# Bias rows of a two-block model, written in 24 pieces during the first layer's feed-forward

## The reference

```
s = einsum(q, k) * Dh**-0.5 + bias[rel_pos];  masked;  softmax
```

## Time and profile before

| | |
|---|---|
| median of 3 runs | 1955.09 us |
| lowest, highest | 1953.01, 1956.92 us |
| profiled execution | 1958.29 us |
| its span | 1955.80 us |
| TensorE busy | 1879.0 us (96%) |
| VectorE busy | 1169.9 us (60%) |
| ScalarE busy | 884.6 us (45%) |
| GpSimd busy | 90.3 us (5%) |
| mean granted TensorE clock | 0.988 |

### The profile page before, as it was taken

How to read it: one execution, slowest core, us unless ns; L and a number is a source line. 1 busy time by engine, 2 the same in 40 slices (tenths; PEclk the granted TensorE clock), 3 DMA queues, 4 the chain that set the end, 5 groups by cost and what they waited for, 6 DMA issues and landing times.

```text
span 1955.8 us, 22425 instructions
## 1 busy us (share of the span) xinstructions
PE 1879.0 (96%) x9135; PEld 1546.6 (79%) x9135; DVE 1169.9 (60%) x1352; ACT 884.6 (45%) x1063; POOL 90.3 (5%) x108
## 2 busy tenths in 40 slices
PE   7999999999869999999999999999999999999997
PEld 5887888877758888888877778887888877778886
DVE  4777554757845557456566575456556566575445
ACT  5545444556434445344345444444344345444442
POOL 5220000022200000000000000000000000000000
PEclk9989999999989999999999999999999999999999
DMA  7414655543755555664455654566563455654562
GB/s 244 157 44 142 193 188 175 195 168 120 105 177 193 174 182 214 200 195 148 145 164 179 233 187 131 192 208 233 179 215 128 145 184 175 233 172 145 182 221 98
DMA packets 194277, 340.47 MB, mean 174 GB/s; under 512 B 9214, under 2 KB 59294, under 8 KB 194176
## 3 DMA queue, kind: packets, MB, share of 16 engines
q1 hardware_dynamic: 188944, 327.76, 50.7%
q0 software_dynamic: 5232, 11.29, 3.2%
HBM read 333.24 MB, written 5.77 MB: 173 GB/s over the span
## 4 chain that ended last, share of the span: by engine, by line
PE 84%; DVE 7%; ACT 3%; DVEq 2%; DMA 2%; issue 1%; SPq 0%; ACTq 0%
PE G L679 18%; PE G L680 18%; PE G L684 18%; PE T L732 5%; PE A L679 4%; PE A L680 4%; PE A L684 4%; PE G L700 2%; PE G L694 2%; PE G L695 2%; DVE wlo L1653 1%; DMA gains<-in_norm_post_mlp 1%; PE T L781 1%; PE A L694 1%; ACT whi L1195 1%
## 5 line engine op out<-in xcount | busy, mean ns | idle before, releaser
L1653 DVE TENSOR_TENSOR wlo<-raw,whi 128x2048 fp32r<-128x2048 f32 (+3 forms) x292 | 629.7, 2158 | 532.6 <-ACT whi L1195 532.3
L1195 ACT ACTIVATE whi<-raw 128x2048 fp32r<-128x2048 f32 (+3 forms) x292 | 525.3, 1801 | 544.6 <-PE G L684 477.9
L679 PE MATMUL G<-whi,XH 128*128 128x512 f32 (+1 forms) x1408 | 557.4, 396 | 4.8 <-DVE XL L1667 3.5
L680 PE MATMUL G<-whi,XL 128*128 128x512 f32 (+1 forms) x1408 | 547.2, 389 | 0.0
L684 PE MATMUL G<-wlo,XH 128*128 128x512 f32 (+1 forms) x1408 | 346.2, 388 | 0.0
L679 PEld LDWEIGHTS G<-whi,XH 128*128 128x128 f32 x1408 | 264.5, 188 | 60.1 <-DVE XL L1667 4.3
L680 PEld LDWEIGHTS G<-whi,XL 128*128 128x128 f32 x1408 | 264.6, 188 | 53.4 <-issue 1.9
L684 PEld LDWEIGHTS G<-wlo,XH 128*128 128x128 f32 x1408 | 263.9, 188 | 53.6
L732 PE MATMUL T<-ident,arena 128*128 128x128 f32 x804 | 115.7, 284 | 14.6 <-ACT arena L1195 7.9
L732 PEld LDWEIGHTS T<-ident,arena 128*128 128x128 f32 x804 | 95.5, 145 | 34.2 <-issue 12.6
L1195 ACT ACTIVATE arena<-T 128x512 f32<-128x512 f32 (+2 forms) x92 | 46.0, 550 | 158.0 <-PE T L732 158.0
(11 more groups left out here) (243 smaller groups left out, 2264.1 us busy)
## 6 DMA issues: line engine op xcount, KB each, us to landing
raw<-in_w_in SPq DMA_DIRECT2D x112, 1024.0 KB, 7.4
raw<-in_w_mlp_up SPq DMA_DIRECT2D x32, 1024.0 KB, 5.2
raw<-in_w_mlp_down SPq DMA_DIRECT2D x32, 1024.0 KB, 5.0
raw<-in_w_ffn_gate SPq DMA_DIRECT2D x44, 512.0 KB, 4.0
raw<-in_w_ffn_up SPq DMA_DIRECT2D x44, 512.0 KB, 5.1
raw<-in_w_out SPq DMA_DIRECT2D x16, 1024.0 KB, 5.0
raw<-in_w_ret_proj SPq DMA_DIRECT2D x16, 1024.0 KB, 5.1
raw<-in_w_ffn_down SPq DMA_DIRECT2D x28, 512.0 KB, 3.6
```

The source lines that it names most:

```text
L679: nc.tensor.matmul(dst(m), hx[:, k0 + k, rows], hi[:, k, :], start=first and k == 0, stop=False)
L680: nc.tensor.matmul(dst(m), lx[:, k0 + k, rows], hi[:, k, :], start=False, stop=False)
L1195: return nc.scalar.activation(out_, in_, func, **kw)
L1653: tt(lo_, raw[:, slot, 0:n], hi.bitcast(F32), ALU.subtract).then_inc(part_sem(blk, c, s_lo, s_lo1), 1)
```

## The change

The three DMAs behind both layers of block 1 are replaced by 24 DMAs inside layer 0, after its rotary embeddings. Piece n writes 16 of the 128 copies of one group of six rows (192 KB), and waits until TensorE has used unit `U_MLP + n` (18 to 41) of layer 0. The groups take turns: g = 0, 1, 2, 0, ... Then GpSimd waits for all 24 and loads the decay table, and goes on to layer 1. What is written, and where, is the same.

```diff
 RQ0 = 3 * ATTN_W
 SEG1 = 7
+PIECES = 8
...
                 rope(pool, nc.gpsimd, RTP, D_Q, 4, HD, 0).then_inc(s_prope.sem, 1)
                 pool.drain()
-
-            pool.wait_ge(s_bvec, 1)
-            for g in range(3):
-                pool.dma_start(bias_rows[g::3], rowsb_of(g).unsqueeze(1).to_broadcast([HG, P, 512])).then_inc(s_brow, 16)
-            pool.wait_ge(s_brow, 48)
-            pool.dma_start(decay[:], a["c_decay"]).then_inc(s_dec, 16)
+                if L == 0:
+
+                    pool.wait_ge(s_bvec, 1)
+                    for n in range(3 * PIECES):
+                        pool.wait_ge(s_used.sem, s_used.at(0, L, U_MLP + n + 1))
+                        g, p0 = n % 3, P // PIECES * (n // 3)
+                        pool.dma_start(bias_rows[g::3, p0:p0 + P // PIECES],
+                                       rowsb_of(g).unsqueeze(1).to_broadcast([HG, P // PIECES, 512])).then_inc(s_brow, 16)
+                    pool.wait_ge(s_brow, 48 * PIECES)
+                    pool.dma_start(decay[:], a["c_decay"]).then_inc(s_dec, 16)
+
             for L in range(DEPTH):
```

## The result

| | before | after |
|---|---|---|
| median | 1954.8 us (4 runs) | 1936.38 us (4 runs) |
| lowest, highest | 1953.01, 1956.92 | 1935.19, 1939.31 |
| profiled execution, its span | 1958.29, 1955.80 | 1937.44, 1935.4 |

The ratio is 0.9905, with a 95% interval of 0.9889 to 0.992: 16 to 22 us won. Forecast were 1938.2 us and 16.85 us. Lines of the changed kernel are one higher than before up to GpSimd's part and six higher behind it (L1195 is L1196, L1653 is L1659).

A forecast was written before the change was run, and what follows sets the result against it. The prediction took TensorE's stall after layer 1's attention, its loads crowded by slow writes, as the bound. Removing the writes there gains 16.85 us, the added pieces cost zero: 1955.09 - 16.85 = 1938.2 us, range 1933.5 to 1943.

The forecast's parts named there:

- What bounds the kernel: After layer 1's attention in block 1, TensorE waits 15.8 us because its loads share DMA engines with 4.6 MB of slow writes.
- 16.85 us by layer 0's measure: Layer 1's stretch of 151 matmuls should fall from 48.35 us to layer 0's 31.50, saving 16.85 us.
- forecast's own range: 1934.5 to 1941 us for the main forecast, from the spread of runs and up to 1 us more or less; chance 0.82.
- Added issues: 24 DMAs in layer 0's MLP cost GpSimd 27 us of issue at 1.1 us each, hidden before layer 1's rope.
- DMA room: In layer 0's MLP, evenly spread pieces and weight loads fill 4.80 of each 5.67 us, 85%; a piece costs 25.2 engine-us.
- Slack of 13.3 us: In layer 0's MLP a weight load is wanted 18.4 us after issue, leaving 13.3 us against a piece's 4.2.
- Rival 1: TensorE's clock may drop in layer 1's attention: 4.0 us more, 1942.2 us; chance 0.08.
- Rival 2: Pieces on the same six engines starve layer 0's MLP: 29 us lost, 1967 us; chance 0.03 full, 0.05 partial.
- Rival 3: Layer 1's late loads were caused by one another, so the stall stays: 1955 us, no change; chance 0.02.
- The Trainium skill's rule: A copy runs on at most as many engines as its slowest dimension allows, here six; GpSimd's copies take consecutive engines from a cursor.
- The row beside it: Three such copies filled 94.9% of sixteen engines before the change; a fixed set of six could have filled only 37.5%.

The follow-up runs named there:

- x2_pieces_old_place: Against the changed kernel: the same 24 pieces of 192 KB, issued without waits between them at the old place after layer 1's rope; 1946.62 us, ratio 0.9965.
- x8_layer1_mlp: Against the changed kernel: the same 24 pieces, paced alike, but in layer 1's MLP; 1936.54 us, ratio 0.9916.
- x5_six_of_768: Against the changed kernel: the same bytes in six DMAs of 768 KB, one every fourth unit of layer 0's MLP; 1965.41 us, ratio 1.0053.
- x7_four_a_unit: Against the changed kernel: the same 24 pieces, four at a time in the first six units of the MLP; 1949.95 us, ratio 0.9989.
- x10_two_rows_and_14: Against the changed kernel: 18 two-row pieces of 256 KB, one per unit, each followed by a useless 14-row copy; 1958.0 us, ratio 1.0032.
- x9_two_rows: Against the changed kernel: 18 pieces of 256 KB, each two rows by 64 copies, one per unit of layer 0's MLP; 1955.74 us, ratio 1.0017.
- x3_same_six: Against the changed kernel: a useless 10-row copy of 16 bytes a row behind each piece, on the same queue; 1934.57 us, ratio 0.9898.

## Why the prediction was right

- *What bounds the kernel.* Right: the stall of layer 1 was crowding by the writes. x2_pieces_old_place leaves them at the old place and keeps 8.5 us of TensorE's wait; x8_layer1_mlp moves them elsewhere and saves as much as the change.
- *16.85 us by layer 0's measure.* Right: the stretch went from 48.35 to 31.50, and the stage from 258.39 to 241.49, 16.90. The medians moved by 18.4, in an interval of 16 to 22, which holds 16.85. Whether the other 1.6 us belong to the change is open; the first column of the table spreads by more. (The forecast's own range should begin at 1935.2 and not 1934.5 us by its own words, 1953.01 - 16.85 less 1; the measured 1936.38 lies in both.)
- *Added issues.* GpSimd's issues cost 0.60 us each, not 1.1; hidden both ways. The first two pieces came 2.35 us apart (186.24 and 188.59 us) and overlapped, the others about 5.7 apart as forecast; it cost nothing.
- *DMA room.* 85% was forecast and 79% measured. A piece cost (0.229 x 140 x 16 - 26) / 24 = 20.3 engine-us and not 25.2, with an estimate of 26 for the decay load (0.52 MB at the 49.3 of the weights). With it a weight load was late by 2.9 us at most of the median (5.1 to 8.0), and 9.0 at the worst, under the 9.3 of the sum.
- *Slack of 13.3 us* (18.4 from issue to use, less a landing of 5.1). Borne out by three sizes: landings up to 13.3 us cost nothing, where most land past 18.4 it costs 23 us.
- *Rival 1, the clock.* It did not come in the changed kernel, but it is real: x5_six_of_768 and x7_four_a_unit pay 124.1 us for layer 1's attention where the changed kernel pays 120.05, 4.0 us as forecast. The low level (0.50, 1.2 GHz) holds for 3.4 us there in the changed kernel (first line), after 6.8 us of which TensorE was busy for 5.98, and in x5_six_of_768 for 13.7 us (second line), after 13.4 with 10.90 busy, and 3.4 more. x10_two_rows_and_14 has 10.3 and 3.4 us of it and takes 122.53. That the changed kernel was spared may be luck: no run shows what decides it.

```profile
516.80:520.20 3.40, 3.38 (x15) 2.93 (x16) 2.73 (x7) 1.75 (x3) 0.00 (x0) 0.50 0.00 0
522.40:536.10 13.70, 13.67 (x64) 11.40 (x64) 8.55 (x23) 3.91 (x15) 0.00 (x0) 0.50 0.01 2
```

- *Rival 2, slower.* Its mechanism was made to happen: big pieces (x5_six_of_768), fast pieces (x7_four_a_unit) and narrow ones (x9_two_rows) take back 14 to 29 us. The change escapes with 192 KB on six engines once in 5.67 us. Its full form, every piece on the same six engines, is ruled out by two pieces in flight that took 59.8% of the engines and moved more bytes a us than one; six engines are 37.5%.
- *Rival 3.* Fell: the loads land in 6.1 to 7.2 us once the writes are gone.
- *The Trainium skill's rule* ("DMA: Bandwidth & Descriptors", on why a DMA increments its semaphore by 16): the half on few engines agrees with x9_two_rows. On the half about a cursor, which I let decide between forecast and rival, the runs are divided: six-row pieces do move on to other engines (34.0%, then 59.8%), but x3_same_six and x10_two_rows_and_14, built to bring each piece back to the same engines, did not do so. The row beside it, 94.9% of 16 engines busy, had carried the argument by itself.

## What to carry to other kernels

A write nobody waits for still takes DMA time from a load that somebody waits for; put it where the loads have slack, and compute the slack as issue to use less issue to landing. Then hold three things under it: the size of one piece, the number of pieces per load, and the number of rows, since few rows mean few engines. Where the program has a twin stretch without the suspect, take its length for the forecast: here it was right to a hundredth of a us for the stretch.

## What the runs showed of the hardware

A 1 MB load lands after 5.1 us alone, 8.0 beside pieces of 192 KB, 10.7 beside 384 KB, 20.7 beside 768 KB (medians), and after 20.9 beside 256 KB in two rows: the number of rows counts as well as the bytes. Writing 4.6 MB in 24 pieces at once (x2_pieces_old_place) took 53.9 us from the first issue to the last landing, where three DMAs took 72.0. And layer 0's MLP comes out at 251.88 to 251.96 us in seven kernels, without writes or with up to 384 KB a piece in it, while the start-up spreads by 5.8 us and layer 1's attention takes 119.07 to 124.09 us, mostly by how long the low clock lasts in it: comparing stages tells differences that totals hide.
